# Three pairs of output tiles of an output projection, formed from seven block products each

## What is computed

```python
D_MODEL = 1024
MLSTM_INNER = 2 * D_MODEL
...
    hn = jnp.transpose(hn, (0, 2, 1, 3)).reshape(B, T, MLSTM_INNER) * outnorm_w.astype(jnp.float32)
    y = (hn.astype(x.dtype) + skip * xc) * jax.nn.silu(z)
    return x + y @ w_out, C, n, m, new_buf
```

## Time and profile before

| | us |
|---|---|
| median of 3 runs | 1073.77 |
| lowest and highest | 1072.58, 1074.06 |
| the profiled execution | 1073.0 |
| its span, first to last instruction | 1071.2 |
| TensorE busy | 1046.5 |
| VectorE, ScalarE, GpSimd busy | 484.8, 259.8, 235.6 |
| tiles 2 to 7 of stage C, 602.41 to 705.77 | 103.36 |

### The profile page before, as it was taken

The page is one execution under the profiler, slowest core; times in us unless marked ns, Lnnn a source line. Parts: engine busy times, 40 slices in busy tenths (PEclk is TensorE's granted clock), DMA queues, the critical chain, the costliest instruction groups (busy, mean ns, idle before and its releaser), DMA issues.

```text
span 1071.2 us, 12431 instructions
## 1 busy us (share of the span) xinstructions
PE 1046.5 (98%) x4528; PEld 678.5 (63%) x4528; DVE 484.8 (45%) x1127; ACT 259.8 (24%) x539; POOL 235.6 (22%) x310
## 2 busy tenths in 40 slices
PE   7999999999989999999999999999999999999997
PEld 5677777777754453634546777777766666656667
DVE  7955444444457575775753010125323333343225
ACT  3212121211244233233321000011223323242220
POOL 5742333324014123341312010101110100100000
PEclk9999999999989999999999999999999999999999
DMA  7224331433294989979798121212210111212202
GB/s 263 96 77 153 114 127 67 148 132 108 93 347 181 352 290 363 375 308 341 297 373 301 67 79 39 78 59 101 89 62 26 56 40 62 93 37 72 78 16 99
DMA packets 44639, 162.27 MB, mean 151 GB/s; under 512 B 4844, under 2 KB 9196, under 8 KB 35632
## 3 DMA queue, kind: packets, MB, share of 16 engines
q1 hardware_dynamic: 44592, 161.65, 41.7%
HBM read 104.42 MB, written 57.21 MB: 151 GB/s over the span
## 4 chain that ended last, share of the span: by engine, by line
PE 65%; DVE 4%; POOL 1%; ACT 0%; issue 0%; DVEq 0%; POOLq 0%
PE work_b L642 16%; PE work_a L642 12%; PE work_a L969 6%; PE work_b L1150 5%; PE work_a L866 3%; PE bank L936 3%; PE work_b L919 2%; PE work_a L1220 2%; PE bank L1195 2%; DVE arena L2049 1%; PE bank L1325 1%; PE work_a L1180 1%; PE work_a L945 1%; PE bank L1198 1%; PE work_a L1293 1%; PE bank L1210 1%
## 5 line engine op out<-in xcount | busy, mean ns | idle before, releaser
L2049 DVE SCALAR_TENSOR_TENSOR arena<-arena,bank 128x512 f32<-128x512 f32 x128 | 87.1, 743 | 63.6 <-PE bank L936 63.6
L642 PE MATMUL work_b<-arena,ring 128*128 128x320 f32 x384 | 107.6, 433 | 0.0
L642 PEld LDWEIGHTS work_b<-arena,ring 128*128 128x128 f32 x384 | 71.5, 190 | 27.8
L642 PE MATMUL work_a<-xc,ring 128*128 128x320 f32 x256 | 70.4, 434 | 0.6 <-POOL xc L2401 0.6
L642 PE MATMUL work_b<-xc,ring 128*128 128x320 f32 x256 | 69.6, 432 | 0.0
L969 PE MATMUL work_a<-arena 128*128 128x512 f32 x128 | 64.4, 615 | 2.8 <-ACT arena L1484 2.8
L739 PE MATMUL work_a<-arena 128*128 128x320 f32 x224 | 64.9, 433 | 0.6 <-DVE arena L1819 0.6
L739 PE MATMUL work_a<-arena,ring 128*128 128x320 f32 x224 | 64.9, 433 | 0.4 <-DVE arena L1767 0.4
L739 PE MATMUL work_b<-arena 128*128 128x320 f32 x224 | 62.6, 432 | 0.0
L642 PEld LDWEIGHTS work_a<-xc,ring 128*128 128x128 f32 x256 | 48.3, 190 | 22.3 <-POOL xc L2401 1.1
L642 PEld LDWEIGHTS work_b<-xc,ring 128*128 128x128 f32 x256 | 48.6, 190 | 20.3
(11 more groups left out here) (312 smaller groups left out, 1691.4 us busy)
## 6 DMA issues: line engine op xcount, KB each, us to landing
ring<-in_stream SPq DMA_DIRECT2D x66, 512.0 KB, 3.5
arena<-in_c SPq DMA_DIRECT2D x32, 1024.0 KB, 8.0
out_s_c<-arena SPq DMA_DIRECT2D x32, 1024.0 KB, 5.4
v_scratch<-arena SPq DMA_DIRECT2D x16, 320.0 KB, 4.3
k_scratch<-arena SPq DMA_DIRECT2D x16, 320.0 KB, 3.4
z_scratch<-arena SPq DMA_DIRECT2D x16, 320.0 KB, 3.5
arena<-k_scratch SPq DMA_DIRECT2D x4, 1280.0 KB, 12.1
arena<-z_scratch SPq DMA_DIRECT2D x4, 1280.0 KB, 9.4
```

Of the source, the lines that this page charges most:

```text
L642: done = mm(halves(buf)[:, a, :], lhs, rhs[:, a * HALF:(a + 1) * HALF], start=first, stop=last)
L2049: op = v.scalar_tensor_tensor(ct[s % CS][:, g, :], ct[s % CS][:, g, :], decb[:, h, b:b + 1], bank[g][:, :], ALU.mult, ALU.add)
```

## The change

Tiles 0 and 1 are formed as before. For each of the pairs m = 1, 2, 3 (tiles 2m, the upper one, and 2m + 1, the lower one) the weights are a 2 x 2 matrix of blocks, one ring slot each: slots 0 and 1 for the upper tile, 2 and 3 for the lower. The inputs are a 2 x 2 matrix too: upper or lower eight inner tiles, left or right half of the tokens. In place of the eight block products of the plain form, seven are formed (Winograd's variant of Strassen's scheme), each of eight matmuls of 128x320, in this order on TensorE:

| product | weights | inputs | to |
|---|---|---|---|
| first | slot 0 | upper, left | work_a |
| second | slot 1 | lower, left | bank 0 |
| fourth | slot 3 | `y_mix[3]` | bank 1 |
| sixth | `o_mix[1]` | `y_mix[1]` | bank 2 |
| fifth | `o_mix[0]` | `y_mix[0]` | bank 3 |
| seventh | `o_mix[2]` | `y_mix[2]` | work_b, first half |
| third | `o_mix[3]` | lower, right | work_b, second half |

`y_mix` are four mixed inputs of 128x2560 each, formed once by VectorE. `o_mix` are four mixed weights of 128x1024, formed for each pair by GpSimd. ScalarE copies the first product to SBUF, and VectorE adds the products into the four quarters of the two tiles of `x1`. SyncE loads slots 0, 2 and 3 again when the sixth product is done and slot 1 when the fifth is. The lower tile of a pair is finished before the upper one, and the consumers follow that order (`out_tile_order`). The loops of the stage are written out on every engine.

```diff
-            def stage_c(m):
-                for s in range(SLOTS):
-                    load_weight((m + 1) * SLOTS + 2 * NI + s, s, C.fill[s // 2] if s % 2 == 0 else None)
-            c.rounds(KD // 2, stage_c)
+            for s in range(SLOTS):
+                load_weight(2 * NI + SLOTS + s, s, C.fill[s // 2] if s % 2 == 0 else None)
+            for m in range(1, OUT_PAIRS):
+                sp.wait_ge(prod_mm, out_product(m, SIXTH))
+                for s in (0, 2, 3):
+                    load_weight(2 * NI + (m + 1) * SLOTS + s, s, None)
+                sp.wait_ge(prod_mm, out_product(m, FIFTH))
+                load_weight(2 * NI + (m + 1) * SLOTS + 1, 1, None)
...
+            def out_block(dst, weights, tokens_of, raised):
+
+                for k in range(KD):
+                    last = mm(dst[:, 0:HALF], weights[:, k, :], tokens_of[:, k, :], start=k == 0, stop=k == KD - 1)
+                last.then_inc(raised, c.up(raised))
+
+            def out_pair(m):
+                first = m == 1
+                if first:
+                    pe.wait_ge(C.free[0], c.all(C.free[0]))
+                else:
+                    pe.wait_ge(prod_kept, c.all(prod_kept))
+                pe.wait_ge(w_in[0], c.next(w_in[0], step=16))
+                out_block(quarter[0], ring[:, 0], xc[:, 0:KD, 0:HALF], prod_mm)
...
+                if first:
+                    pe.wait_ge(y_mixed, 4)
+                pe.wait_ge(w_in[3], c.next(w_in[3], step=16))
+                c.skip(w_in[2], 1, 16)
+                out_block(bank[1], ring[:, 3], y_mix[3], prod_mm)
+                pe.wait_ge(pool_mixed, c.all(pool_mixed, ahead=3))
+                out_block(bank[2], o_mix[1], y_mix[1], prod_mm)
+                pe.wait_ge(pool_mixed, c.all(pool_mixed, ahead=4))
+                c.skip(pool_mixed, 4)
+                out_block(bank[3], o_mix[0], y_mix[0], prod_mm)
+                pe.wait_ge(C.free[1], c.all(C.free[1]))
+                out_block(quarter[2], o_mix[2], y_mix[2], C.fill[1])
+                pe.wait_ge(C.free[0], c.all(C.free[0]))
+                out_block(quarter[3], o_mix[3], xc[:, KD:NI, HALF:T], C.fill[0])
...
+            for m in range(1, OUT_PAIRS):
+                act.wait_ge(prod_mm, out_product(m, FIRST))
+                nc.scalar.activation(o1_kept, quarter[0], ACT.Copy).then_inc(prod_kept, c.up(prod_kept))
+                square_tile(2 * m + 1)
+                square_tile(2 * m)
...
+            dve.wait_ge(y_ready, 2 * HEADS)
+            mix_y(0, xc[:, 0:KD, right], xc[:, 0:KD, left])
+            dve.wait_ge(y_mixed, 1)
+            mix_y(1, xc[:, KD:NI, right], y_mix[0])
+            out_tile(0)
+            dve.wait_ge(misc_in, 16 * 9)
+            dve.wait_ge(y_mixed, 2)
+            mix_y(3, xc[:, KD:NI, left], y_mix[1])
+            mix_y(2, xc[:, KD:NI, right], xc[:, 0:KD, right])
+            out_tile(1)
...
+                add_to(x1[:, 2 * m:2 * m + 2, right], both(o4))
+                dve.wait_ge(C.fill[1], c.next(C.fill[1]))
+                dve.wait_ge(dve_own, c.all(dve_own))
+                add_to(two(low_tile), both(quarter[2]), C.free[1])
+                dve.wait_ge(C.free[1], c.all(C.free[1]))
+                scaled_x(2 * m + 1)
+                dve.wait_ge(C.fill[0], c.next(C.fill[0]))
+                add_to(top_tile[:, right], quarter[3], C.free[0])
+                dve.wait_ge(C.free[0], c.all(C.free[0]))
+                scaled_x(2 * m)
...
+            def mixed_out_weights(m):
+                if m > 1:
+                    pool.wait_ge(prod_mm, out_product(m - 1, FIFTH))
+                done = MIXED_A + 4 * (m - 1)
+                for slot in (2, 3):
+                    pool.wait_ge(w_in[slot], 16 * (NI // 2 + 1 + m))
+                g.tensor_tensor(o_mix[0], ring[:, 2], ring[:, 3], ALU.add).then_inc(pool_mixed, 1)
+                pool.wait_ge(w_in[0], 16 * (NI // 2 + 1 + m))
+                pool.wait_ge(pool_mixed, done + 1)
+                g.tensor_tensor(o_mix[1], o_mix[0], ring[:, 0], ALU.subtract).then_inc(pool_mixed, 1)
+                if m > 1:
+                    pool.wait_ge(C.fill[1], m)
+                g.tensor_tensor(o_mix[2], ring[:, 0], ring[:, 2], ALU.subtract).then_inc(pool_mixed, 1)
```

More of the change, by code:

```diff
@@ L409, in program, with out_product @@
         own_pad = [take(2 * P - STEP) for _ in range(2)]
+        PROD_A, MIXED_A = 5 * (NI - 2), 4 * (NI - 2) + 2
+        FIRST, SECOND, FOURTH, SIXTH, FIFTH = range(1, 6)
+        OUT_PAIRS = KD // 2
+        out_tile_order = [0, 1] + [n for m in range(1, OUT_PAIRS) for n in (2 * m + 1, 2 * m)]
+        def out_product(m, which):
+            return PROD_A + 5 * (m - 1) + which
         def leave(c):
@@ L580, in _ @@
                 sp.dma_start(dst, i[name]).then_inc(misc_in, c.up(misc_in, 16))
-            def stage_c(m):
-                for s in range(SLOTS):
-                    load_weight((m + 1) * SLOTS + 2 * NI + s, s, C.fill[s // 2] if s % 2 == 0 else None)
-            c.rounds(KD // 2, stage_c)
+            for s in range(SLOTS):
[6 more added lines that the diff above has]
+                load_weight(2 * NI + (m + 1) * SLOTS + 1, 1, None)
+            for s in range(2):
+                c.skip(C.fill[s], OUT_PAIRS - 1)
             at = 2 * NI + 2 * KD + SLOTS
@@ L1038, in _ @@
             pe.wait_ge(small_out, 2 * HEADS)
-            def stage_c(m):
-                for s in range(2):
[L1043 to L1055, removed]
+            for q in range(2):
+                c.skip(w_in[q], 1, 16)
@@ new lines, in _ @@
+            c.skip(C.fill[0])
+            c.skip(C.free[0])
+            for q in range(NI):
+                if q % KD == 0:
+                    pe.wait_ge(w_in[2 + q // KD], c.next(w_in[2 + q // KD], step=16))
+                last = tokens(work[1], ring[:, 2 + q // KD, q % KD, :], xc[:, q, :], q == 0, q == NI - 1)
+            last.then_inc(C.fill[1], c.up(C.fill[1]))
+            c.skip(C.free[1])
+            def out_block(dst, weights, tokens_of, raised):
+                for k in range(KD):
+                    last = mm(dst[:, 0:HALF], weights[:, k, :], tokens_of[:, k, :], start=k == 0, stop=k == KD - 1)
+                last.then_inc(raised, c.up(raised))
@@ L1056, in stage_c @@
                     c.skip(C.free[s])
-            c.rounds(KD // 2, stage_c)
-            pe.wait_ge(C.free[0], c.all(C.free[0]))
+            for m in range(1, OUT_PAIRS):
+                out_pair(m)
+            pe.wait_ge(prod_kept, c.all(prod_kept))
             pe.wait_ge(w_in[0], c.next(w_in[0], step=16))
-            for k in range(KD):
+            for k in out_tile_order:
                 pe.wait_ge(normed, c.next(normed))
-                last = tokens(work[0], ring[:, 0, k, :], xk[:, k, :], k == 0, k == KD - 1)
+                last = tokens(work[0], ring[:, 0, k, :], xk[:, k, :], k == out_tile_order[0], k == out_tile_order[-1])
@@ L1530, in _, with square_tile @@
                     weigh_k(h + 1)
[L1533 to L1538, removed]
+            def square_tile(n):
+                s = n % 2
+                act.wait_ge(C.free[s], c.next(C.free[s]))
+                op = nc.scalar.activation(gate[:, n, :], x1[:, n, :], ACT.Square)
+                op.then_inc(squares, c.up(squares))
+            square_tile(0)
+            square_tile(1)
+            for m in range(1, OUT_PAIRS):
+                act.wait_ge(prod_mm, out_product(m, FIRST))
+                nc.scalar.activation(o1_kept, quarter[0], ACT.Copy).then_inc(prod_kept, c.up(prod_kept))
+                square_tile(2 * m + 1)
+                square_tile(2 * m)
             def latent(n):
@@ L2120, in _ @@
                 dve.wait_ge(c_out[s], 16 * HEADS * STEPS // CS)
[L2122 to L2130, removed]
@@ L2131, in _, with mix_y, scaled_x, out_tile @@
-            c.rounds(KD // 2, stage_c)
+            left, right = slice(0, HALF), slice(HALF, T)
+            def mix_y(q, a, b):
+                v.tensor_tensor(y_mix[q], a, b, ALU.subtract).then_inc(y_mixed, c.up(y_mixed))
+            def scaled_x(n):
+                op = v.tensor_scalar(xk[:, n, :], x1[:, n, :], vec[:, V_KN + n:V_KN + n + 1], None, ALU.mult)
+                op.then_inc(normed, c.up(normed))
+            def out_tile(s):
+                dve.wait_ge(C.fill[s], c.next(C.fill[s]))
+                x = two(x1[:, s, :])
+                v.tensor_tensor(x, x, halves(work[s]), ALU.add).then_inc(C.free[s], c.up(C.free[s]))
+                dve.wait_ge(C.free[s], c.all(C.free[s]))
+                scaled_x(s)
@@ new lines, in _, with add_to @@
+            dve.wait_ge(y_ready, 2 * HEADS)
[8 more added lines that the diff above has]
+            out_tile(1)
+            def add_to(x, part, raised=None):
+                raised = raised or dve_own
+                v.tensor_tensor(x, x, part, ALU.add).then_inc(raised, c.up(raised))
```

62 lines of the change are left out of this document (55 added, 7 removed).

## The result

The changed kernel takes **1061.45 us** in the median of 4 runs (1059.82 to 1064.99), against 1073.59 for the kernel before beside it (1072.58 to 1074.06): ratio 0.9887, 95% interval 0.9866 to 0.9907. The forecast was 1060.9. The profiled execution took 1060.94 us, its span is 1059.1.

The account below looks back on a forecast made before the run. TensorE, busy back to back in the output projection, was taken as the bound. Span 1071.2 - 12.9 = 1058.3 us, plus 1.8 for the execution and 0.8 for the median: 1060.9 us, range 1059.4 to 1064.2.

Parts of the forecast that it names:

- The removed matmuls: Output projection, three pairs: 168 written matmuls in place of 192, at 0.538 us each, 12.9 us less.
- second rival: At all 21 products TensorE pays 0.24 us for its wait: 5.0 us in all, 1065.9 us; chance 0.05.
- The rest of the program: Behind the stage: all is chained by waits, with no transfer of absolute date, so the gain should reach the end.
- fourth rival: Behind the stage: a late transfer or new wait loses about half the gain, 1067 us; chance 0.03.
- VectorE's mixed inputs: Beside tile 1: four of 128x2560, 3.3 to 5.7 us each, last done near 600.6, due at 611.02, cost nothing.
- Four times 0.83: Lower price of one VectorE mixed input, 3.3 us: four times the 128x640 row with two SBUF operands.
- GpSimd's mixed weights: Four of 128x1024 per pair, 2.4 us each; in pair 1 three done by 614.2, due at 615.33.
- the upper price of 3.7: One GpSimd mix while both engines work in SBUF: pair 1's three done by 617.9, a stall of 2.6 us.
- first rival: Pair 1's sixth product: mixed weights come late, stall 0.3 to 2.6 us, up to 3.6, typically 1062.9 us; chance 0.17.
- The room of 1.1 us: Pair 1's sixth product: time to spare between GpSimd's third mix at 614.2 and its due time, 615.33.
- Slots for the next pair: Slots 0, 2 and 3 loaded 2.2 us after the fifth product ends; slot 0 due only 12.9 us after it.
- The end of the stage: Last tile scaled 1.4 us after the last product, due at 7.5; squares ran to 3.6, due at 8.6.

Follow-up runs that it names:

- after: The changed kernel in its first comparison against the kernel before: 1061.45 us in the median of 4 runs, against 1073.59, ratio 0.9887.
- e0: The changed kernel again, nothing altered, beside runs of the kernel before on another chip: 1063.06 us of 4 runs, ratio to before 0.9898.
- e9: The changed kernel once more, nothing altered, on the chip of the version with six filler matmuls: 1061.60 us of 5 runs, ratio to before 0.9877.
- e4_late1: The changed kernel with one more GpSimd mix of 128x1024 ahead of pair 1's third; profile only: 457.6 us from tile 1's end, against 455.9.

## Why the prediction was right

The mechanism is the one forecast: TensorE's chain got shorter by the matmuls left out, and everything added was ready before it was due. That is shown by the profiles.

**The removed matmuls.** 12.9 us forecast, 12.92 measured in the stage, and 12.9 when the eighth product is put back. Nothing is paid at a product's start: second rival (5 us) refuted.

**The rest of the program.** Forecast: the gain reaches the end. The part behind the stage is 365.4 us in both, so the fourth rival is refuted.

**VectorE's mixed inputs.** Priced at 3.3 to 5.7 us each; they took 2.83. Four times 0.83 was too much: if the time is a fixed part and a part per column, the two rows (640 columns 0.83, 2560 columns 2.83) give a fixed part of 0.16 us, an estimate, which one wide instruction pays once and four narrow ones four times. Begun at 582.73 (forecast 582.6), the last ended at 597.2 (forecast 600.6); 2.4 of these 3.4 us come from the loads, behind which the third mix began at 591.58 and not at 594.

**GpSimd's mixed weights.** Priced at 2.4, measured 2.34 to 2.38 in pair 1 and up to 2.6 in the others. The interpolation between two widths held, and the upper price of 3.7, that of both engines at work in SBUF, came up nowhere. What was mis-sized is the start. The forecast let the mixes begin where the loads' traffic ends, 4.3 us behind tile 1's end (606.75 against 602.41), with 0.1 for a dependent start; the first one began 5.1 behind it (608.34 against 603.22). The traffic stopped 4.5 us behind the tile's end, 0.2 later than in the earlier trace rows, and 0.6 us passed between its end and GpSimd's first mix, a term that the sum put at nothing and only the first rival named:

```profile
607.50:607.75 0.25, 0.25 (x3) 0.17 (x2) 0.00 (x0) 0.19 (x1) 0.00 (x0) 1.00 0.08 33
607.75:608.00 0.25, 0.25 (x3) 0.17 (x2) 0.00 (x0) 0.25 (x1) 0.00 (x0) 1.00 0.00 0
```

The room of 1.1 us was thus 0.6. (The forecast's own terms, 606.75 + 7.2 + 0.1, end at 614.05 and not at its 614.2, so its room should have read 1.3; the later start took 0.8 of that.) Had the loads come 0.7 us later still, it would have been the first rival's stall, which had a chance of 0.17.

**Slots for the next pair.** The forecast has slot 0 due 12.9 us after the fifth product. It is due 12.9 us after the sixth ends and 8.6 after the fifth; with the load in place 2.2 us after the fifth, nothing hung on it.

**The end of the stage.** The last tile was scaled 1.1 us after the last product (forecast 1.4) and the squares were summed 2.9 us after it (3.6), both due at 7.5 and 8.6.

**The level.** 1060.9 forecast, 1061.45 measured. That the two are so close is in part luck: the single runs lie 1.6 us below the median and 3.5 above it, the highest (1064.99) outside the forecast range, and the same code came out 12.1, 11.0 and 14.2 us under before in its three comparisons (after, e0, e9). The stage gives 12.9 each time; the rest is ahead of it, in every profile. The range had been widened for late weights, which did not come; that executions differ by several us through the clock near 300 us was not in the forecast, although show its fall.

## What to carry to other kernels

Where the chain is one engine back to back, the gain is the count of what is left out, and the work goes into showing a due time for each added operation. The place to look at is the first use: later turns have a whole turn's lead, the first has only what was loaded or computed ahead of the loop. A missed due time there costs a little more than its length while the clock holds, 1.7 us for a stall of 1.5, and much more where the clock falls, 12.3 us for a stall of 9.1. How long a stall between these two may be was not measured.

## What the runs showed of the hardware

VectorE's scaling of a tile, 128x640 with one tile of SBUF read, took 0.55 us alone and 2.02 beside GpSimd's mixes, of which the next took 2.60 instead of 2.35:

```profile
629.27 2.36 POOL L2565 TENSOR_TENSOR arena<-arena,ring 128x1024 f32<-128x1024 f32 x1
...
629.95 2.02 DVE L2196 TENSOR_SCALAR arena<-arena,vec 128x640 f32<-128x640 f32 x1
...
631.59 2.60 POOL L2568 TENSOR_TENSOR arena<-ring 128x1024 f32<-128x1024 f32 x1
```

Without the mixes, at the same place, it takes 0.55 (GpSimd's cut mix is over in 0.21):

```profile
631.20 0.21 POOL L2568 TENSOR_TENSOR arena<-ring 128x8 f32<-128x8 f32 x1 [1.85 <-PE work_b L1081]
...
632.01 0.55 DVE L2196 TENSOR_SCALAR arena<-arena,vec 128x640 f32<-128x640 f32 x1
```

I had looked for this between instructions with two SBUF inputs only and had not counted the scaling among them. The Trainium skill (SBUF — State Buffer, Who interferes with whom) names `tensor_scalar` too among the operations that can enter a mode which takes the ports that both engines share, and says that whoever comes second waits for the whole instruction of the other. The trace agrees roughly: the mix at 629.27 had 1.7 us left when the scaling began, and with 0.55 that makes 2.2 for the 2.02 measured. It cost nothing here, since nobody waits for the scaled tile before the end, where GpSimd is done with mixing.

A gap on TensorE costs a little more than the idle time that the profile shows, even at the full clock: behind the 1.47 us of e4_late1 (granted clock 1.00) the two products took 8.88 us, 0.27 more than elsewhere. Of this, 0.16 is how the idle time is counted: at full pace a product's records begin 0.16 us before those of the one ahead end (615.98 against 616.14 in the changed kernel), and a gap is counted from that end. About 0.1 us is left.
